# Stick-breaking attention: softplus in one ScalarE pass, later keys' sums from a rounded part and a rest

## What is computed

```python
z = jnp.einsum("bhqd,bhkd->bhqk", qi, kh).astype(jnp.float32) * scale
mask = kpos[None, :] < qpos[:, None]
sp = jnp.where(mask, jax.nn.softplus(z), 0.0)
rev = lax.cumsum(sp, axis=3, reverse=True)
w = jnp.exp(jnp.where(mask, z - rev, -jnp.inf))
out = jnp.einsum("bhqk,bhkd->bhqd", w.astype(v.dtype), vh)
```

## Time and profile before

| what | value |
|---|---|
| median of 3 runs | 3475.7 us (3475.01 to 3485.14) |
| the profiled execution | span 3475.7 us |
| busy, share of the span | PE 98%, PEld 78%, DVE 44%, ACT 40%, POOL 41% |
| the chain that ended last | PE 87%, DVE 6%, ACT 5%, POOL 1% |
| end of the last `EV` product to start of the output product | 2438.4 to 2496.2 us |

### The profile page before, as it was taken

One profiled execution on the slowest core, in us unless ns is written; L12 is line 12 of the kernel. 1 busy time (PEld: TensorE's weight loads), 2 busy tenths in 40 slices (PEclk: granted clock), 3 DMA queues, 4 the chain that ended last, 5 costly groups with the idle time before them and its releaser, 6 DMA issues.

```text
span 3475.7 us, 39071 instructions
## 1 busy us (share of the span) xinstructions
PE 3397.2 (98%) x15914; PEld 2708.7 (78%) x15914; DVE 1535.6 (44%) x2252; ACT 1377.3 (40%) x2281; POOL 1409.0 (41%) x759
## 2 busy tenths in 40 slices
PE   7999999999999999999999999999999999999999
PEld 5887667887888788776787788876678887778887
DVE  3436664345332343756435433556456412543320
ACT  3545444324232444545422433254742324643221
POOL 2333444544444433344444444433344444134443
PEclk9999999999999999999999999999999999999999
DMA  6334212444554333421254455332135533113332
GB/s 223 103 114 130 61 49 61 139 134 148 171 167 127 108 104 109 134 55 49 61 146 144 142 173 167 108 99 67 37 107 174 152 96 107 41 55 109 97 90 74
DMA packets 566993, 385.31 MB, mean 111 GB/s; under 512 B 13606, under 2 KB 504310, under 8 KB 566814
## 3 DMA queue, kind: packets, MB, share of 16 engines
q1 hardware_dynamic: 564574, 379.58, 37.3%
q10 hardware_dynamic: 2240, 3.25, 0.3%
HBM read 379.27 MB, written 2.10 MB: 110 GB/s over the span
## 4 chain that ended last, share of the span: by engine, by line
PE 87%; DVE 6%; ACT 5%; POOL 1%; issue 1%; DMA 0%; SPq 0%; DVEq 0%; POOLq 0%; ACTq 0%
PE ps L179 85%; PE ps L183 2%; DVE mq L154 1%; ACT L138 1%; ACT whi L142 1%; DVE NUM L146 1%; POOL wlo L146 1%; ACT sp L138 1%; DVE H L154 0%; ACT UF L138 0%; DMA W<-in_w_ada 0%; ACT xr L138 0%; DVE mq L151 0%; SPq L176 0%; DVE G L163 0%
## 5 line engine op out<-in xcount | busy, mean ns | idle before, releaser
L146 POOL TENSOR_TENSOR wlo<-raw,whi 128x1024 fp32r<-128x1024 f32 (+1 forms) x540 | 1257.7, 2338 | 1828.7 <-ACT whi L142 1753.2
L179 PE MATMUL ps<-UH,whi 128*128 128x512 f32 x2656 | 1057.0, 398 | 7.6 <-ACT UH L138 4.8
L179 PE MATMUL ps<-UL,whi 128*128 128x512 f32 x2656 | 1037.0, 391 | 4.0 <-POOL UL L146 3.2
L179 PE MATMUL ps<-UH,wlo 128*128 128x512 f32 x2656 | 1038.1, 391 | 0.0
L142 ACT ACTIVATE whi<-raw 128x1024 fp32r<-128x1024 f32 (+1 forms) x540 | 548.5, 1025 | 750.8 <-PE ps L179 355.4
L179 PEld LDWEIGHTS ps<-UH,whi 128*128 128x128 f32 x2656 | 501.0, 189 | 130.9 <-issue 13.9
L179 PEld LDWEIGHTS ps<-UL,whi 128*128 128x128 f32 x2656 | 500.1, 188 | 115.0 <-POOL UL L146 6.6
L179 PEld LDWEIGHTS ps<-UH,wlo 128*128 128x128 f32 x2656 | 501.2, 189 | 109.0 <-issue 5.7
L179 PE MATMUL ps<-GH,whi 128*128 128x512 f32 x704 | 275.3, 391 | 0.0
L179 PE MATMUL ps<-GL,whi 128*128 128x512 f32 x704 | 274.0, 389 | 0.0
L179 PE MATMUL ps<-GH,wlo 128*128 128x512 f32 x704 | 273.9, 389 | 0.0
(11 more groups left out here) (372 smaller groups left out, 4187.0 us busy)
## 6 DMA issues: line engine op xcount, KB each, us to landing
raw<-in_w_in SPq DMA_DIRECT2D x168, 512.0 KB, 3.9
raw<-in_w SPq DMA_DIRECT2D x120, 512.0 KB, 5.3
raw<-in_ada_w SPq DMA_DIRECT2D x96, 512.0 KB, 5.0
raw<-in_w_ada SPq DMA_DIRECT2D x80, 512.0 KB, 4.8
raw<-in_ffn_w_gate SPq DMA_DIRECT2D x44, 512.0 KB, 4.0
raw<-in_ffn_w_up SPq DMA_DIRECT2D x44, 512.0 KB, 3.9
raw<-in_ffn_w_down SPq DMA_DIRECT2D x32, 512.0 KB, 3.9
raw<-in_ev_w_in SPq DMA_DIRECT2D x20, 512.0 KB, 3.9
```

The lines of the kernel that those rows point to most:

```text
L146: return self.e.tensor_tensor(o, a, b, op).then_inc(*self.done(*keys))
L179: m = self.e.matmul(o, l, r, start=start, stop=stop)
```

## The change

- GpSimd gets a new pass for each head, `bounded`: min(z, 30) over 1280 columns into `sp` (key `zc`). It stands behind the mask of the pair.
- ScalarE's `soft` becomes one Softplus over `sp` in place (key `sf`), and later a copy of the finished tile rounded to fp32r into `sph` (key `sph`), both over 1280 columns.
- VectorE's `sums` becomes `full`: max(z, sp), two SBUF inputs, 1280 columns.
- A new pass `split_rest` subtracts the rounded copy from the tile: on VectorE for even heads, on GpSimd for odd ones (keys `sp` of dve and pool, the same tile under the name `sl`).
- `later_keys` multiplies both parts in fp32r by `TO`, a copy of the triangle and the ones that two new ScalarE copies make at the layer's start: twenty matmuls of one instruction each.
- There are three `sp` tiles where there were six, and three `sph`. Heads use them as 0, 1, 2, 0, 1, 2, 1, 2; so `bounded` of heads 3 to 7 waits until `later_keys` of heads 0, 1, 2, 4, 5 is through.

```diff
+    SP_AT = (0, 1, 2, 0, 1, 2, 1, 2)
+    def sp_before(h):
+        return {3: 0, 4: 1, 5: 2, 6: 4, 7: 5}.get(h)
...
+    def split_rest(e, h):
+        e.wait_ge(*on("act", "sph", h))
+        e.tt(sp_of(h, "sl")[:, :], sp_of(h)[:, :], sp_of(h, "sh")[:, :].bitcast(F32), ALU.subtract, ("sp", h))
...
         def later_keys(h):
-            sp = sp_of(h)
-            p.wait_ge(*on("dve", "sp", h))
+            hi, lo, TO = sp_of(h, "sh"), sp_of(h, "sl"), EV["TO"]
+            p.wait_ge(*on("act", "to"))
+            p.wait_ge(*on("act", "sph", h))
             for kb in range(4):
                 n = 512 - 128 * kb
                 o = bank(p, (4, 5, 6), ("su", h, kb), ("dve", ("su", h, kb)))
-                for k2 in range(kb, 4):
-                    p.mm(o[:, 128 * (k2 - kb):n], tri if k2 == kb else ones, sp[:, OFF[k2]:OFF[k2 + 1]], k2 == kb, k2 == 3,
-                         *([("su", h, kb)] if k2 == 3 else []))
+                for x in (hi, lo):
+                    if x is lo:
+                        p.wait_ge(*on(rest_lane(h), "sp", h))
+                    for k2 in range(kb, 4):
+                        p.mm(o[:, 128 * (k2 - kb):n], TO[:, 0:128] if k2 == kb else TO[:, 128:256], x[:, OFF[k2]:OFF[k2 + 1]],
+                             x is hi and k2 == kb, x is lo and k2 == 3, *([("su", h, kb)] if x is lo and k2 == 3 else []))
...
+        a.cp(EV["TO"][:, 0:128], tri)
+        a.cp(EV["TO"][:, 128:256], ones, "to")
...
         def soft(i):
             for x in range(2):
                 h = 2 * i + x
-                a.wait_ge(*on("pool", "zm", h))
-                if h > 5:
-                    a.wait_ge(*on("pe", "su", h - 6, 3))
-                a.af(sp_of(h)[:, :], EV["zs"][h][:, :], ACT.Abs, ("ab", h))
+                a.wait_ge(*on("pool", "zc", h))
+                a.af(sp_of(h)[:, :], sp_of(h)[:, :], ACT.Softplus, ("sf", h))
             for x in range(2):
                 h = 2 * i + x
-                a.wait_ge(*on("act", "ab", h))
-                a.af(sp_of(h)[:, :], sp_of(h)[:, :], ACT.Exp, ("ex", h), scale=-1.0)
-            for x in range(2):
-                h = 2 * i + x
-                a.wait_ge(*on("act", "ex", h))
-                a.af(sp_of(h)[:, :], sp_of(h)[:, :], ACT.Ln, ("ln", h), bias=1.0)
+                a.wait_ge(*on("dve", "sf", h))
+                if sp_before(h) is not None:
+                    a.wait_ge(*on("pe", "su", sp_before(h), 3))
+                a.cp(sp_of(h, "sh")[:, :], sp_of(h)[:, :], ("sph", h))
...
-        def sums(h):
-            z, sp = EV["zs"][h], sp_of(h)
-            v.wait_ge(*on("act", "ln", h))
-            v.stt(sp[:, :], z[:, :], 0.0, sp[:, :], ALU.max, ALU.add, ("sp", h))
+        def full(h):
+            v.wait_ge(*on("act", "sf", h))
+            v.tt(sp_of(h)[:, :], EV["zs"][h][:, :], sp_of(h)[:, :], ALU.max, ("sf", h))
...
+        def bounded(h):
+            g.wait_ge(*on("pool", "zm", h))
+            if sp_before(h) is not None:
+                g.wait_ge(*on("pe", "su", sp_before(h), 3))
+            g.ts(sp_of(h)[:, :], EV["zs"][h][:, :], SOFT_END, None, ALU.min, None, ("zc", h))
...
+            if i:
+                split_rest(g, 2 * i - 1)
+            bounded(2 * i)
+            bounded(2 * i + 1)
+        split_rest(g, 7)
```

More of the change, by code:

```diff
@@ L2424, in program, with sp_of, rest_lane @@
                  [at(f"zs{4 + i}", 68 + 5 * i, [128, 1280], F32, BASE) for i in range(4)],
[L2425 to L2430, removed]
+              sp=[at(f"sp{i}", (8, 72, 89)[i], [128, 1280], F32, BASE if i == 2 else ARENA) for i in range(3)],
+              sl=[at(f"sl{i}", (8, 72, 89)[i], [128, 1280], F32R, BASE if i == 2 else ARENA) for i in range(3)],
+              sh=[at(f"sph{i}", (24, 77, 94)[i], [128, 1280], F32R, BASE if i == 2 else ARENA) for i in range(3)],
+              TO=at("TO", 94.5, [128, 256], F32R))
+    SOFT_END = 30.0
+    SP_AT = (0, 1, 2, 0, 1, 2, 1, 2)
+    def sp_before(h):
+        return {3: 0, 4: 1, 5: 2, 6: 4, 7: 5}.get(h)
+    def sp_of(h, part="sp"):
+        return EV[part][SP_AT[h]]
+    def rest_lane(h):
+        return "pool" if h % 2 else "dve"
+    def split_rest(e, h):
+        e.wait_ge(*on("act", "sph", h))
+        e.tt(sp_of(h, "sl")[:, :], sp_of(h)[:, :], sp_of(h, "sh")[:, :].bitcast(F32), ALU.subtract, ("sp", h))
     def qk_of(a):
@@ L2724, in less @@
                 v.wait_ge(*on("pe", "su", h, kb))
-                v.wait_ge(*on("dve", "sp", h))
                 v.tt(z[:, c], z[:, c], ps(("su", h, kb))[:, 0:n], ALU.subtract, ("su", h, kb))
@@ L2742, in dve_even @@
         scores(1, (0, 1))
-        sums(0)
+        full(0)
+        full(1)
+        split_rest(v, 0)
         scores(1, (2, 3))
-        sums(1)
         copy_ev(v)
@@ L2748, in dve_even @@
         scores(2, (0, 1))
-        sums(2)
+        full(2)
+        full(3)
         less(1)
+        split_rest(v, 2)
         scores(2, (2, 3))
-        sums(3)
         less(2)
+        full(4)
         scores(3, (0, 1))
+        full(5)
         less(3)
-        sums(4)
+        split_rest(v, 4)
         scores(3, (2, 3))
-        sums(5)
         less(4)
         out_tile(0)
+        full(6)
         less(5)
-        sums(6)
-        sums(7)
+        full(7)
+        split_rest(v, 6)
         less(6)
```

## The result

| | changed kernel | kernel before |
|---|---|---|
| median of the runs shown | 3493.4 us (3489.6 to 3499.1) | 3475.8 us (3475.0 to 3485.1) |
| ratio, 95% interval | 1.0046 (1.0034 to 1.0058) | |
| the profiled execution | span 3497.3 us | span 3475.7 us |
| the stage: last score product ahead of `later_keys(0)` to the output product | 2442.99 to 2519.83, 76.8 us | 2438.49 to 2496.20, 57.7 us |

The changed kernel is about 0.5% slower, 16 us by the ratio and 17.6 by the medians. The stage holds the loss: it is 19.1 us longer. (One of the six runs of the changed kernel was disturbed, at 9136 us; it is left out of the range and the ratio, and without it the median is 3492.5 us.) The profiled execution was the longest of the other five.

What follows compares the result with a forecast made beforehand. TensorE was taken to bound the kernel, with ScalarE also nearly full in the attention stage. 3475.7 + 2.7 (chain through four engines) + 3.5 (TensorE's half clock) = 3481.9 us; range of 8 in 10: 3473 to 3490.

Steps and rivals of the forecast that it cites:

- What bounds the kernel now: Attention stage: TensorE and ScalarE nearly full; only the output product's start ends it; differences under about 0.3% can't be told.
- What is taken away: Attention: later_keys falls from 4.60 to 2.8 us a head; ScalarE loses one pass of three and three table loads.
- What is added: VectorE gets four rests of 1.48 us; GpSimd four rests of 2.95 and eight bound passes of 1.25 us.
- the price b of the bound pass: GpSimd's min(z, 30) over 1280 columns: taken as 1.25 us, with no trace row of its own.
- the upper bound: Ceiling on the bound pass's GpSimd price: the two-input subtraction's 2.95 us.
- The place: Attention: a chain crossing four engines once a pair delays the output product, plus 2.7 us.
- third named wait of TensorE: TensorE's wait before values(3), forecast at 3.2 us.
- the rival's own sum: If the bound pass costs 2.95 us: 8 x 1.7 = 13.6 on the chain, about 1.4 hidden; 2.7 + 12.2 + 3.5.
- TensorE's clock: Attention: half clock behind TensorE's waits costs 0 to 8.6 us; 3.5 was taken.
- The sum: Whole kernel: 3475.7 + 2.7 for the chain + 3.5 for the clock = 3481.9 us.
- the bound pass is dear: Rival: GpSimd's bound pass costs 2.95 us, putting all eight on the chain; 3494 us, chance 0.14.
- the range to 3490: Whole kernel's time: range of 8 in 10, from 3473 to 3490 us.

Runs made afterwards that it cites:

- no_bound: Changed kernel without its eight bound passes, Softplus reading the masked score itself: 3477.0 us, ratio to the kernel before 1.0003.
- softplus_only: Changed kernel without rounded copy, rests and fp32r products; keeps bound pass, Softplus and larger-of, with fp32 sums as before: 3485.8 us, ratio to the kernel before 1.0025.
- bound_dve: Changed kernel with the bound passes moved from GpSimd to VectorE, whose order also changed: 3479.4 us, ratio to the kernel before 1.0012.
- folded: Changed kernel with the bound folded into VectorE's larger-of behind Softplus, less ahead of full, and fp32 sums as before: 3470.9 us, ratio to the kernel before 0.9986.
- folded_split: Changed kernel with the bound folded into VectorE's larger-of and less ahead of full, keeping the fp32r split: 3472.4 us, ratio to the kernel before 0.9990.
- less_first: Changed kernel with only VectorE's order changed, less ahead of the next full, bound passes still on GpSimd: 3484.6 us, ratio to the kernel before 1.0025.
- bound_twice: Changed kernel with each bound pass done twice, the second behind the first: 3526.1 us, one run.
- split_only: Changed kernel with the old Abs, Exp, Ln softplus and no bound pass, keeping the fp32r split; less(5) ahead of full(6): 3498.4 us, ratio to before 1.0062.
- fill2: Changed kernel with 24, 42 and 20 unused filler products in TensorE's waits ahead of later_keys(1), (3), (5) last blocks: 3494.7 us, ratio to before 1.0060.

## Why the prediction was wrong, point by point

**What bounds the kernel now**: right. Only this stage changed, and only the start of the output product counts: it is 19.1 us later within the stage, and the medians differ by 17.6. That under 0.3% nothing can be told was too careful: the interval of the result is 0.12% to either side.

**What is taken away**: right. `later_keys` without waits takes 3.0 us of TensorE (2485.89 to 2488.9 for head 4) against the 2.8 put together from the earlier trace rows, at full clock:

```profile
2485.89 0.85 PE L179 MATMUL ps<-sph,TO 128*128 128x512 f32 x4
2486.58 0.80 PE L179 MATMUL ps<-sl,TO 128*128 128x512 f32 x4
...
2488.49 0.28 PE L179 MATMUL ps<-sph,TO 128*128 128x128 f32 x1
2488.61 0.27 PE L179 MATMUL ps<-sl,TO 128*128 128x128 f32 x1
```

The 128-column products start 0.12 us apart, as taken. The program has 100 table loads for 103, and ScalarE is no longer the pacemaker, as was said (41.5 of 76.8 us busy).

**What is added**: here is the step that failed, the price b of the bound pass. The rests were right (2.93 for 2.95; VectorE's 1.48). The bound pass was put "small as the memset is" at 1.25 us, between 1.17 and 2.95. It takes 3.44, outside the bounds, and its eight passes are worth 20.8 us of stage (`no_bound`). Two things went wrong. The choice followed the number of inputs, a rule for which the rows had two instances, a memset and a mask, neither with a constant in an arithmetic operation. And the upper bound rested on the same rule: that one input can't cost more than two. The copy shows that the number of inputs is not it. For an instruction kind without a row in the trace, the two-input row was no bound.

**The place**: right. The chain through GpSimd, ScalarE, VectorE, the bank and TensorE is the one in the traces, with its waits where they were named and longer: 7.24 us for 5 before Softplus(2), 4.4 and 8.0 for 4.0 and 6 in TensorE. Only the third named wait of TensorE is shorter, 1.67 us for 3.2 before `values(3)`. With 3.44 for 1.25 the rival's own sum, 8 x 2.19 less the 1.4 hidden and plus 2.7, gives +18.8 us where the stage showed +19.1. Laid out before each run, the same durations gave -3.7 to -0.2 without the passes where the stage showed -1.6; it gave +7.5 for +8.0 in `softplus_only`, +2 to +4 for +3.6 in `bound_dve`, -5.4 for -4.7 in `folded`, and -6.4 to -1.1 for -5.5 in `folded_split`. Its misses are `less_first` (2 too long), `bound_twice` (2.2 too short) and `split_only` (3 too short).

**TensorE's clock**: 3.5 us were added. `values(0)` was at half as foreseen, 3.73 us for 2.38, `values(3)` (2.37 us) and the output product were not, and `values(1)`, which I had not listed, was (3.96 us). `fill2` gives 1.1 us for 20 of the 34 us at half. There was far more half clock than I had listed, and it was worth less. That most of it ran beside GpSimd's work, and so cost nothing, is the likely reason; the remaining 14 us were not tried.

**The sum**: 2.7 + 3.5 became 18.8 + about 1.1, 19.9 for the measured 19.1. The rival "the bound pass is dear" had the mechanism, the place and the sign, at 3494 against 3493.4 measured, and a chance of 0.14. It hit by two errors against each other: b at 2.95 is too small by 0.5, and the clock too large. The chance was too small for what the rows said, since an operation with no row of its kind, eight times on the chain, has its price as the main unknown, and the range to 3490 cut off the end that b = 2.95 gives.

## What to carry to other kernels

Before a pass is moved to an idle engine, price that kind of instruction there: GpSimd was idle three quarters of the stage, and one form of instruction, not its share, decided. A bound or other constant goes into a VectorE instruction that is there anyway (min and max in one, 1.49 us for 1.48) at no cost. And in an engine's fixed order, what frees a bank for another engine goes ahead of what waits for a third: moving `less` ahead of `full` gave 10.6 us of the stage with the same work.

## What the hardware showed that I had not expected

- GpSimd: tensor and constant 2.55 ns a column plus 0.2 us (3.44 us at 1280, fp32), alike for smaller-of, sum and product at 640; two constants 2357 ns at 640 columns against 1816 with one; two tensors 1542; copy 1249 at 1280. VectorE does the same bound pass in 0.82 us.
- A VectorE pass that meets a long GpSimd pass shows the wait as its own duration, not as idle time: 2.89 to 3.08 us for 1.5 with two SBUF inputs, 2.98 for 0.82 with one and a constant. In the changed kernel this happened three times, and each time VectorE's pass ended 0.9 us after GpSimd's. In the group of `sp<-zs,sp` the mean was 2074 ns in the changed kernel and 1509 without the bound passes:

```profile
L146 DVE TENSOR_TENSOR sp<-zs,sp 128x1280 f32<-128x1280 f32 x8 | 16.6, 2074 | 16.6 <-ACT sp L138 16.6
```
```profile
L146 DVE TENSOR_TENSOR sp<-zs,sp 128x1280 f32<-128x1280 f32 x8 | 11.9, 1509 | 3.9 <-ACT sp L138 3.9
```

- Half clock cost little in this stage, which waits for other engines: 20 us less of it were worth 1.1 us.
